# Weight slabs split in place: one ring of four raw/low slots and four high slots, in a two-block transformer kernel on one core

## What is computed

```python
# first block
mod = silu(c) @ ada_w + ada_b                       # shift, scale, gate
h = rms_norm(x, norm_g) * (1 + scale) + shift
proj = h @ w_in                                     # 9 segments of 1024 columns, and 80 index columns
o_a = sparse_attention(...) * silu(a_g)             # 8 heads, top 64 keys
o_r = rms_norm(hgrn2_recurrence(...)) * silu(r_g)   # 8 heads, chunks of 64
x = x + gate * (concat(o_a, o_r) @ w_out)
# second block, two layers
x = x + rmsnorm(pool_mixer(rmsnorm(x), w_pool))     # layer 0
x = x + rmsnorm(swiglu(rmsnorm(x), w_gate, w_up, w_down))
kv = rmsnorm(x) @ w_kv                              # layer 1: differential attention
q = rmsnorm(x) @ w_q
x = x + rmsnorm(diff_attention(q, kv) @ w_o)
x = x + rmsnorm(swiglu(...))
```

## Time and profile before

| what | value |
|---|---|
| median of 3 runs (lowest to highest) | 2760.87 us (2760.17 to 2760.97) |
| span of the profiled execution, first to last instruction | 2756.0 us |
| TensorE busy | 2610.5 us, 95% of the span |
| VectorE busy | 1416.6 us, 51% |
| ScalarE busy | 1117.2 us, 41% |
| GpSimd busy | 310.5 us, 11% |
| read from memory | 502.01 MB, 183 GB/s over the span |
| mean granted clock of TensorE | 0.973 of full |

### The profile page before, as it was taken

The page is one execution under the profiler, slowest core; times in us unless marked ns, Lnnn a source line. Parts: engine busy times, 40 slices in busy tenths (PEclk is TensorE's granted clock), DMA queues, the critical chain, the costliest instruction groups (busy, mean ns, idle before and its releaser), DMA issues. The chain is left out here.

```text
span 2756.0 us, 31637 instructions
## 1 busy us (share of the span) xinstructions
PE 2610.5 (95%) x11812; PEld 2101.0 (76%) x11812; DVE 1416.6 (51%) x1286; ACT 1117.2 (41%) x1046; POOL 310.5 (11%) x271
## 2 busy tenths in 40 slices
PE   5799999997987999999999999998989999999997
PEld 1388888855876888888888778887778888888886
DVE  6764435457456444444444455576454444444444
ACT  4634323334344343343333344454443434333332
POOL 7100059901002000000000002200010000000000
PEclk8899999998989999999999999999999999999999
DMA  8845536553524554646546455543445655555463
GB/s 288 330 159 192 177 138 228 190 176 108 198 87 156 185 204 161 214 162 217 207 160 229 168 165 195 190 146 133 173 153 184 197 183 185 196 183 214 161 221 122
DMA packets 185620, 505.31 MB, mean 183 GB/s; under 512 B 17680, under 2 KB 17968, under 8 KB 184128
## 3 DMA queue, kind: packets, MB, share of 16 engines
q1 hardware_dynamic: 183472, 493.63, 51.5%
q0 software_dynamic: 1536, 8.37, 1.0%
q10 hardware_dynamic: 528, 2.16, 0.2%
HBM read 502.01 MB, written 2.10 MB: 183 GB/s over the span
## 5 line engine op out<-in xcount | busy, mean ns | idle before, releaser
L1281 DVE TENSOR_TENSOR lo<-raw,hi 128x2048 fp32r<-128x2048 f32 (+1 forms) x390 | 916.7, 2351 | 1022.8 <-ACT hi L932 1022.2
L932 ACT ACTIVATE hi<-raw 128x2048 fp32r<-128x2048 f32 (+1 forms) x390 | 744.9, 1910 | 1145.2 <-PE acc L502 1109.6
L500 PE MATMUL acc<-hi,h_hi 128*128 128x512 f32 (+1 forms) x2688 | 1057.4, 393 | 31.6 <-DVE h_lo L1351 11.2
L502 PE MATMUL acc<-hi,h_lo 128*128 128x512 f32 (+1 forms) x2688 | 1049.8, 391 | 0.0
L501 PE MATMUL acc<-lo,h_hi 128*128 128x512 f32 (+1 forms) x2688 | 1049.3, 390 | 0.0
L500 PEld LDWEIGHTS acc<-hi,h_hi 128*128 128x128 f32 x2688 | 510.3, 190 | 141.4 <-DVE lo L1281 19.7
L502 PEld LDWEIGHTS acc<-hi,h_lo 128*128 128x128 f32 x2688 | 509.8, 190 | 105.7
L501 PEld LDWEIGHTS acc<-lo,h_hi 128*128 128x128 f32 x2688 | 510.7, 190 | 102.4
L500 PE MATMUL acc<-hi,g_hi 128*128 128x512 f32 x704 | 274.0, 389 | 0.0
L502 PE MATMUL acc<-hi,g_lo 128*128 128x512 f32 x704 | 273.9, 389 | 0.0
L501 PE MATMUL acc<-lo,g_hi 128*128 128x512 f32 x704 | 273.9, 389 | 0.0
(11 more groups left out here) (282 smaller groups left out, 1378.1 us busy)
## 6 DMA issues: line engine op xcount, KB each, us to landing
raw<-in_w_ffn_gate SPq DMA_DIRECT2D x176, 512.0 KB, 3.8
raw<-in_w_ffn_up SPq DMA_DIRECT2D x176, 512.0 KB, 4.7
raw<-in_w_ffn_down SPq DMA_DIRECT2D x176, 512.0 KB, 4.1
raw<-in_w_in SPq DMA_DIRECT2D x144, 512.0 KB, 4.3
raw<-in_ada_w SPq DMA_DIRECT2D x96, 512.0 KB, 4.9
raw<-in_w_kv SPq DMA_DIRECT2D x64, 512.0 KB, 4.5
raw<-in_w_out SPq DMA_DIRECT2D x32, 512.0 KB, 4.1
raw<-in_w_q SPq DMA_DIRECT2D x32, 512.0 KB, 3.5
```

The lines of the kernel that those rows point to most:

```text
L500: pe.matmul(o, l_hi, w_hi, start=first, stop=False)
L502: mm = pe.matmul(o, l_lo, w_hi, start=False, stop=last)
L932: act.activation(hi_slots[slot][:, 0:st.cols], raw[:, r, 0:st.cols], ACT.Copy).then_inc(hi_made, 1)
L1281: vec.tensor_tensor(lo_slots[slot][:, 0:st.cols], raw[:, r, 0:st.cols], hi_slots[slot][:, 0:st.cols], ALU.subtract).then_inc(slab_split, 1)
```

## The change

The second set of slots goes away, and `lo` is written over the raw slab that it comes from. The same 64 KB now hold four raw/low slots and four `hi` slots, used in turn by a running slab number (`ring0`). So a slot is free only when TensorE has used the slab: SyncE's `load` of slab n waits for `slab_used` of slab n-4, and `conv` of slab n waits only for its landing. `ada` no longer has extra slots. The order on ScalarE and VectorE is now a table: two slabs of the next group or stage are split ahead of an `evac` and two behind it (`slabs_ahead`, `last_ahead`), also where `hold` kept them back before. `split_turned` has slabs 2 and 3 only (none before `o`; for `pool` the two slabs of its second group). In `v` step n splits slab n+4 instead of n+2. Loops over stages with two groups are written out.

```diff
-RAW = 4
-SPLIT = 2
+RING = 4
 SLAB = 2048
-CREDIT = 2 * SPLIT
...
-    raw = at("raw", [P, RAW, SLAB], RAW0)
-    hi = at("hi", [P, SPLIT, SLAB], HI0, F32R)
-    lo = at("lo", [P, SPLIT, SLAB], LO0, F32R)
-    hi_more = at("hi_more", [P, SPLIT, SLAB], A0, F32R)
-    lo_more = at("lo_more", [P, SPLIT, SLAB], A0 + 16, F32R)
+    raw = at("raw", [P, RING, SLAB], RAW0)
+    lo = at("lo", [P, RING, SLAB], RAW0, F32R)
+    hi = at("hi", [P, RING, SLAB], HI0, F32R)
...
+    last_ahead = {
+        "ada": ([(st_in1, 0, 0), (st_in1, 0, 1)], []),
+        "in1": ([(st_small, 0, 0), (st_small, 0, 1)], [(st_in2, 0, 0)]),
+        "small": ([(st_in2, 0, 1)], [(st_in2, 0, 2), (st_in2, 0, 3)]),
+        "in2": ([], []),
+        "out": ([(st_pool, 0, 0), (st_pool, 0, 1)], []),
+        "pool": ([], []),
+        "gu0": ([(st_down0, 0, 0), (st_down0, 0, 1)], [(st_down0, 0, 2), (st_down0, 0, 3)]),
+        "down0": ([(st_k, 0, 0), (st_k, 0, 1)], []),
+        "k": ([(st_q, 0, 0), (st_q, 0, 1)], [(st_q, 0, 2), (st_q, 0, 3)]),
+        "q": ([(st_v, 0, 0), (st_v, 0, 1)], [(st_v, 0, 2), (st_v, 0, 3)]),
+        "o": ([(st_gu1, 0, 0), (st_gu1, 0, 1)], []),
+        "gu1": ([(st_down1, 0, 0), (st_down1, 0, 1)], [(st_down1, 0, 2), (st_down1, 0, 3)]),
+        "down1": ([], []),
+    }
+
+    def slabs_ahead(st, g, last):
+
+        if last:
+            return last_ahead[st.name]
+        if st is st_pool:
+            return [], [(st_gu0, 0, 0), (st_gu0, 0, 1)]
+        return [(st, g + 1, s) for s in (0, 1)], [(st, g + 1, s) for s in (2, 3)]
+
+    def slab_at_turn(st, i):
+
+        return {st_pool: (st_pool, 1, i // 2 - 2), st_o: None}.get(st, (st, 0, i // 2))
...
             else:
-                split = slab_no(st, g, s) - st.back["raw", s] + 1
-                if not isinstance(split, int) or split > 0:
-                    sp.wait_ge(slab_split, split)
...
+                sp.wait_ge(slab_used, slab_no(st, g, s) + 1)
...
-            r, slot = s % RAW, s % st.split_slots
+            r = slot_of(st, g, s)
             act.wait_ge(raw_landed[r], landed_at(st, g, s))
-            act.wait_ge(slab_used, CREDIT + slab_no(st, g, s) - st.back["split", s] + 1)
             if st.gain is None:
-                act.activation(hi_slots[slot][:, 0:st.cols], raw[:, r, 0:st.cols], ACT.Copy).then_inc(hi_made, 1)
+                act.activation(hi[:, r, 0:st.cols], raw[:, r, 0:st.cols], ACT.Copy).then_inc(hi_made, 1)
...
-            def rest(g, after, first=ahead):
-                for s in range(first, st.slabs):
+            def rest(g, last=False):
+                for s in range(RING, st.slabs):
                     conv(st, g, s)
-                wide_ring = st is st_ada and after and after[0] is st
-                if hold and not (after and after[0] is st):
-                    evac(g)
-                    return
-                if after:
-                    conv(*after, 0)
-                if wide_ring:
-                    conv(*after, 1)
-                    conv(*after, 2)
+                before, behind = slabs_ahead(st, g, last)
+                for slab in before:
+                    conv(*slab)
                 evac(g)
-                if after:
-                    conv(*after, 3 if wide_ring else 1)
+                for slab in behind:
+                    conv(*slab)
                 if post:
-                    if after and after[0] is st:
-                        conv(*after, 2)
                     post(g)
...
             for i in range(KT // 2):
-                if i == 0 and st not in (st_o, st_in1, st_out):
-                    conv(st, 0, 0)
-                if i == 4 and st not in (st_o, st_in1, st_out):
-                    conv(st, 0, 1)
-                if i in (4, 6) and st is not st_pool:
-                    conv(st, 0, i // 2)
+                if i in (4, 6) and slab_at_turn(st, i):
+                    conv(*slab_at_turn(st, i))
...
-            if n + 2 < V_STEPS:
-                conv(st_v, (n + 2) // 8, (n + 2) % 8)
+            if n + RING < V_STEPS:
+                conv(st_v, (n + RING) // 8, (n + RING) % 8)
             else:
-                conv(st_o, 0, n + 2 - V_STEPS)
+                conv(st_o, 0, n + RING - V_STEPS)
```

More of the change, by code:

```diff
@@ L98, in plan @@
 def plan(stages):
-    slab, bank_uses, used = 0, [0] * 4, [0] * RAW
-    last = {("raw", r): -RAW + r for r in range(RAW)} | {("split", r): -CREDIT + r for r in range(CREDIT)}
+    slab, place, bank_uses = 0, 0, [0] * 4
     for st in stages:
-        st.slab0, st.bank0, st.raw0 = slab, list(bank_uses), list(used)
-        st.raw_per_group = [sum(1 for s in range(st.slabs) if s % RAW == r) for r in range(RAW)]
+        st.slab0, st.ring0, st.bank0 = slab, place, list(bank_uses)
+        place += st.groups * st.slabs
         if st.direct:
-            used = [u + st.groups * p for u, p in zip(used, st.raw_per_group)]
             bank_uses = [u + 1 for u in bank_uses]
             continue
[L110 to L117, removed]
         slab += st.groups * st.slabs
-        used = [u + st.groups * p for u, p in zip(used, st.raw_per_group)]
         for t in range(st.tiles):
@@ L443, in load @@
                 sp.dma_start(dst, src).then_inc(raw_landed[r], 16)
-        for i, st in enumerate(stages):
-            if st is st_ada:
-                for s in range(st.slabs):
-                    load(st, 0, s)
-                with sp.Fori(1, st.groups) as g:
-                    for s in range(st.slabs):
-                        load(st, g, s)
-            elif st.groups == 1 or st.direct:
+        for st in stages:
+            if st.groups <= 2:
                 for g in range(st.groups):
@@ L509, in run @@
         def run(st):
-            if st.groups == 1 or st is st_pool:
+            if st.groups <= 2:
                 for g in range(st.groups):
@@ L831, in ffn @@
                 product(st_down[l], 0, s)
-            with pe.Fori(1, st_down[l].groups) as g:
-                for s in range(st_down[l].slabs):
-                    product(st_down[l], g, s)
+            for s in range(st_down[l].slabs):
+                product(st_down[l], 1, s)
         ffn(0)
@@ L1288, in conv, with run, rest @@
             ins.then_inc(slab_split, 1)
-        def run(st, evac, post=None, begun=False, between=None, between_at=0, hold=False):
-            ahead = 3 if post else st.split_slots
-            nxt = follow.get(st.name)
-            def rest(g, after, first=ahead):
-                for s in range(first, st.slabs):
-                    conv(st, g, s)
-                wide_ring = st is st_ada and after and after[0] is st
-                if hold and not (after and after[0] is st):
-                    evac(g)
-                    return
-                if after:
-                    conv(*after, 0)
-                if wide_ring:
-                    conv(*after, 1)
-                    conv(*after, 2)
+        def run(st, evac, post=None, between=None, between_at=0):
+            def rest(g, last=False):
+                for s in range(RING, st.slabs):
+                    conv(st, g, s)
+                before, behind = slabs_ahead(st, g, last)
+                for slab in before:
+                    conv(*slab)
@@ L1306, in rest @@
                 evac(g)
-                if after:
-                    conv(*after, 3 if wide_ring else 1)
+                for slab in behind:
+                    conv(*slab)
                 if post:
-                    if after and after[0] is st:
-                        conv(*after, 2)
                     post(g)
-            first = 4 if begun else ahead
-            peeled = min(between_at + 1, st.groups - 1)
+            peeled = st.groups - 1 if st.groups <= 2 else between_at + 1
             for g in range(peeled):
-                rest(g, (st, g + 1), first)
+                rest(g)
```

114 lines of the change are left out of this document (56 added, 58 removed).

## The result

The changed kernel takes 2794.48 us (median; 2791.53 to 2799.21 in four executions), beside 2760.92 us (2760.17 to 2761.22) for the kernel before: ratio 1.0123, 95% interval 1.0111 to 1.0136. That is 33.6 us slower; forecast were 27.

What follows compares the result with a forecast made beforehand. It took TensorE's matmuls as the bound, busy 95% of the span. Costs of 25.9 + 5 + 4.2 + 5 + 2.5 less 15.6 gained gave +27.0 us on 2760.87, so 2787.9 us, range 2771 to 2810.

Steps and rivals of the forecast that it cites:

- The bound: Gate and up: bound by TensorE's matmuls; in plain groups the new ring holds with 6.7 us to spare, costing nothing.
- rival 4: Evictions come late at the 43 group ends, 0.7 us each: +30, 2818 us; chance 0.06.
- v, the steps: Stage v: work behind the later split is delayed; 13 steps take 121.6 us instead of 95.7, +25.9.
- rival 1: The work behind the split is not what TensorE waits for; ends faster, 2752.8 us; chance 0.06.
- v, the clock: Stage v: some six TensorE waits of about 2.47 us lower the granted clock, +5 us, bounds 0 and 12.
- rival 3: Stage v: the clock falls in every step, +22 us instead of +5, 2805 us; chance 0.10.
- End of v: Step 15 of v: squares and norms stand behind the split of o's slab 3, delaying o's turns, +4.2 us.
- ada: Stage ada: slots held through the product, 11.2 us over four slots, just keep the transfers' pace; +5 us, bounds 0 and 16.
- rival 2: Stage ada becomes bound by its slots, 16 us instead of 5, 2799 us; chance 0.14.
- out to pool: Two pool splits ahead of VectorE's last x_evac lengthen the 5.52 us wait for the bands, +2.5 us.
- The gains: Shorter waits for lo -11.1, pool's first evac behind a split -3.0, less half clock -1.5; together -15.6 us.
- The sum: Whole kernel: all costs less the savings give +27.0 us, a median of 2787.9 us, 1.0% slower.

Runs made afterwards that it cites:

- Experiment 3: Changed kernel with ada's low parts in four slots of their own, so a raw slot is free once both parts are split: 2775.15 us.
- experiment 4: Changed kernel with VectorE evicting out's result ahead of the low splits of pool's first two slabs: 2789.91 us.
- experiment 5: Changed kernel with GpSimd's first large multiply held until VectorE has done the low part of ada's second slab: 2793.29 us.
- Experiments 1 and 2: Changed kernel, v splitting two or three slabs ahead: 2752.74, 2752.09 us; or splitting at step's end on both engines, VectorE, ScalarE: 2755.68, 2778.39, 2802.87 us.

## Why the prediction was right, point by point

**The bound.** Right. Between gu0's second wait for `lo` and the turns of x ahead of `k`, 713 us, the traces differ by 0.0 us. So the plain groups lose nothing to the longer hold, evictions behind two splits are in time, and rival 4 falls. The written-out loops cost nothing.

**v, the steps.** Right in mechanism and in size. Worked out were 19.6 us for two steps at the turns; the row shows 19.75. Forecast were 121.6 us and +5 of clock, 126.6 for the 13 steps: the trace after has 133.1, and the traces of experiments 3, 4 and 5, whose `v` is the same code, 127.0, 126.7 and 127.4. The turns of eight heads stand 9.6 to 9.7 us apart in these three, for the 9.6 of the forecast. The waits stand where they were forecast, and also at the scores, for VectorE's mask; the forecast named only the combination behind it. Experiments 1 and 2 show the cause from two sides: a transfer that lands sooner, or work that doesn't stand behind it, takes the loss away. The forecast's rival 1 falls with them.

**v, the clock.** The term was +5, half of what some six waits would cost, with an upper bound of 12. From the second fill to the turns of o TensorE is busy for 115.8 us in 147.3, clock 0.90, beside 101.3 in 105.6, clock 1.00: 14.6 us longer, and the 13 steps are 11.5 us over the 121.6 worked out without the clock. In the three other traces it is 9.4 to 9.7 us of busy time (clock 0.95 and 0.96) and 5.1 to 5.8 us over the 121.6. So the term was right in three traces of four, and the profiled execution of the changed kernel is the fourth, still within the bound. The loss comes in separate stretches, in which the clock is at the lower of its two levels, 1.2 GHz for 2.4. In the 13 steps they add up to 27 us here and to 10 us in each of the other three. There they stand at the wait of 2.8 to 3.1 us in the fills and at one of 2.7 to 3.4 late in the stage, and at none of the waits of 1.3 us. Here three stand at waits of 2.8 to 3.6 us, one behind a wait of 2.0 and one behind a wait of 1.3. Windows of 10 us, TensorE alone:

```profile
1870.00:1880.00 10.00, 7.03 (x26) 0.83 0.32 107
1880.00:1890.00 10.00, 10.00 (x49) 1.00 0.31 106
1890.00:1900.00 10.00, 6.63 (x19) 0.66 0.29 106
1900.00:1910.00 10.00, 10.00 (x47) 1.00 0.29 107
1910.00:1920.00 10.00, 6.43 (x20) 0.66 0.29 105
```

Of eleven windows between 1800 and 1910, eight show 0.97 or 1.00. So rival 3, a fall in every step, did not come. The section "HAM oscillation" of the Trainium skill's "TensorE: Matmul & The Clock Gate" has a loop pay the return to the slow clock every time that it waits for a transfer; its waits are longer than most of these. That would have been the 22 us of rival 3; the rows show the price only now and then, 9 to 15 us in all.

**End of v.** +4.2 forecast, +4.4 measured (+4.3 to +4.5 in the three other traces).

**ada.** This step failed: "That just keeps the pace but with no slack", +5. It is +15.6, what rival 2 gave (16); in the eight traces that hold the slots as the changed kernel does `ada` ends between 146.6 and 150.9, for 132.76 before. The term that was sized wrong is the cycle of a slot, 11.2 us. In the trace after it is 14.6 on average over the slabs of the second and third group. Both transfers of a slab are in 6.7 us after the first was issued, where the forecast took 4.8 from `v`, where nothing else is in the queue; the trace before has 6.3 for the same slabs. The two splits end 4.8 us later, for 4.2, and TensorE is done with the slab 3.0 us behind them, for 1.9, since it comes late from a wait or an `evac`. Over four slots that is 3.6 us a slab, for a pace of 2.9 that the transfers set. So the slots bound the stage, and a queue whose engines worked for 98% of the time can't make up for a pause. Experiment 3 shows it, by taking away the held slot alone.

**out to pool.** +2.5 forecast for the wait for the bands, 5.52 to 7.72 measured: +2.2, and experiment 4 takes just that away. The stage as a whole is 0.2 us shorter, since the wait at 739.47 is gone too.

**The gains.** -15.6 forecast; the table has -3.0 up to the attention, -2.4 in `out` without the longer wait for the bands, -2.4 in pool, -2.2 at gu0, -5.4 at `k`, -3.2 at gu1, and the first part of `v` -1.2: -19.8 in sum. Those of a pair went as forecast (the first gone, 0.7 us left of the second). That `k` gave 1.9 more is the clock: between its turns of x and its second wait for `lo` TensorE is busy 27.4 us for 29.1, clock 0.93 for 0.90. Up to the first attention it is busy 1.7 us less as well. The forecast had 1.5 us of clock in all its gains. The +1.6 in `o` is the clock the other way: TensorE is busy 95.5 us for 92.6, clock 0.91 for 0.96, and a wait for `h_lo` is 1.7 us shorter.

**The sum.** In the two traces +27.0 stands against +41.3. `ada` was 10.6 too small, the steps of `v` with their clock 6.5 (0.1 to 0.8 in the three other traces), `o` 1.6, and the gains were 4.2 too small. The medians, 7.8 us nearer to each other than the profiled executions, make it +33.6. That this lies so near to +27.0 is in part luck: the gains, which were too small for the clock and not for the waits, hid four of the ten microseconds that `ada` was out.

## What to carry to other kernels

A buffer shared by two steps is held for both, so ask in each stage separately what the next transfer is released by. Where matmuls bound the stage the longer hold cost nothing in 713 us; where transfers bound it, each idle moment of the queue was time lost, and a cycle worked out to be just as long as the pace was no cover: it came out 3.4 us longer.

A split for later, ahead of this step's own work, is harmless as long as its slab has landed, or lands before the step's slack is gone: two ahead ScalarE waited once, three ahead 2.6 us at a time, and neither cost TensorE more than 0.3 us. Four ahead in a ring of four the slab's transfer starts only with this step, and the 6.2 us of waiting came through to TensorE. A deeper look-ahead made it worse, not better. The other cure is to put the split at the end of the engine's list, on every engine that hands the work on: on both it gave back the whole loss of `v`, on VectorE alone 16 us of 39, and on ScalarE alone it cost 8 more.

## What the runs showed of the hardware

VectorE's subtraction of two operands and GpSimd's multiply did not run side by side. In the profiled execution after, they started within 0.05 us:

```profile
22.05 7.01 POOL L1826 TENSOR_TENSOR xn<-x 128x4096 f32<-128x4096 f32 x1 [16.15 <-DMA x<-in_x]
22.10 9.11 DVE L1278 TENSOR_TENSOR lo<-raw,hi 128x2048 fp32r<-128x2048 f32 x1 [9.86 <-ACT hi L938]
```

GpSimd's ends at 29.06, VectorE's 2.15 us later, and by itself it takes 2.29: as if it had begun only when GpSimd was done. The rows of experiment 5 show the same for a split that starts in the middle of the multiply: the multiply ends at 31.53, the split 2.14 us later. The page "SBUF — State Buffer" of the Trainium skill, section "SBUF: two separate sides", says the same: a pair of ports that one of the two holds for its whole instruction while the other is blocked. Here it cost the stage nothing that the traces show (experiment 5).

The granted clock differs from one execution to the next where the code and the waits in front are the same. In the first group of pool, behind a wait of 7.6 to 8.2 us, it was 0.77 to 0.91 in ten traces, and the same 144 matmuls took 24.2 to 28.8 us. In `v` the same code was at the lower level for 27 us in one trace and for 10 in three, 6 us of time. A difference of a few microseconds between two single traces is no evidence for an edit until the clock of the stretch is beside it.
